# Three of the nine convolution taps formed on GpSimd and added once by VectorE, in nine of twelve channel blocks

## The reference

```python
def short_conv(x, w, grid):
    B, T, C = x.shape
    w = w.astype(jnp.float32)
    if grid:
        rows = T // GRID_W
        xg = jnp.pad(x.reshape(B, rows, GRID_W, C), ((0, 0), (1, 1), (1, 1), (0, 0)))
        out = sum(xg[:, i:i + rows, j:j + GRID_W, :] * w[i, j] for i in range(3) for j in range(3))
        return out.reshape(B, T, C)
    xp = jnp.pad(x, ((0, 0), (1, 1), (0, 0)))
    return sum(xp[:, j:j + T, :] * w[1, j] for j in range(3))

def rwkv_mixer(r, k, v, lw, la, lg, s0, grid, p):
    ...
    rkv = short_conv(jnp.concatenate([r, k, v], axis=-1), p['rw_conv'], grid)
    r, k, v = jnp.split(rkv, 3, axis=-1)
    g = jax.nn.sigmoid(lg) @ p['rw_g2']
    kk = heads(k * p['rw_k_k'])
    kk = kk * lax.rsqrt(jnp.sum(kk * kk, axis=-1, keepdims=True) + EPS)
```

## Time and profile before

| What | Value |
|---|---|
| Median of 3 runs | 957.44 us |
| Span of the profiled execution | 963.3 us |
| TensorE busy | 868.1 us, 90% of the span |
| VectorE busy | 562.5 us, 58% |
| ScalarE busy | 331.8 us, 34% |
| GpSimd busy | 151.6 us, 16% |
| Stage of the convolutions | about 197 to 386 us of the span |

### The profile page before, as it was taken

The page is one execution under the profiler, slowest core; times in us unless marked ns, Lnnn a source line. Parts: engine busy times, 40 slices in busy tenths (PEclk is TensorE's granted clock), DMA queues, the critical chain, the costliest instruction groups (busy, mean ns, idle before and its releaser), DMA issues.

```text
span 963.3 us, 21505 instructions
## 1 busy us (share of the span) xinstructions
PE 868.1 (90%) x8900; PEld 533.8 (55%) x8900; DVE 562.5 (58%) x935; ACT 331.8 (34%) x583; POOL 151.6 (16%) x296
## 2 busy tenths in 40 slices
PE   2899999999999979888888988899976899999995
PEld 1455455666455436577777877545565444444442
DVE  3424046699986899365665656686244255444467
ACT  3231111142035664566666553122110122222223
POOL 7000111112000106122223420000001000000041
PEclk9999999999999989899999999999955899999998
DMA  9902222224253102112212121961019499999956
GB/s 331 378 23 95 94 88 99 89 88 154 75 188 109 67 1 42 26 21 53 39 37 34 32 38 47 314 254 44 22 54 361 133 328 373 367 371 368 327 126 226
DMA packets 120816, 142.46 MB, mean 148 GB/s; under 512 B 49996, under 2 KB 86280, under 8 KB 120328
## 3 DMA queue, kind: packets, MB, share of 16 engines
q1 hardware_dynamic: 111880, 116.55, 36.9%
q0 software_dynamic: 3744, 13.63, 4.5%
q10 hardware_dynamic: 5088, 10.82, 3.0%
HBM read 122.99 MB, written 18.00 MB: 146 GB/s over the span
## 4 chain that ended last, share of the span: by engine, by line
PE 79%; DVE 10%; DMA 5%; issue 3%; ACT 3%; SPq 0%; ACTq 0%; DVEq 0%; POOLq 0%
PE bank L1972 72%; PE bank L1976 7%; DMA region<-in_w_ada_dram 3%; DVE rk_r L1431 1%; ACT region L949 1%; DMA region<-in_w_in_dram 1%; DMA rk_r<-h_rows_dram,slot_tokens 1%; DVE region L1431 1%; DVE rk_r L1432 1%; DVE cl_b L1890 1%; DVE region L1961 1%; ACT w_sb L949 1%; ACT ada_row_buffers L949 0%; DVE region L1957 0%; DVE region L1943 0%
## 5 line engine op out<-in xcount | busy, mean ns | idle before, releaser
L1972 PE MATMUL bank<-region 64*64 64x64 f32 (+3 forms) x3900 | 402.6, 299 | 16.4 <-issue 6.5
L1972 PEld LDWEIGHTS bank<-region 64*64 64x64 f32 (+1 forms) x3900 | 233.3, 149 | 171.6 <-issue 160.1
L949 ACT ACTIVATE region<-bank 128x256 f32<-128x256 f32 (+3 forms) x216 | 97.8, 453 | 357.7 <-PE bank L1972 261.1
L1972 PE MATMUL bank<-region,rk_r 128*128 128x512 f32 x176 | 81.0, 615 | 0.8 <-issue 0.8
L1976 PE MATMUL bank<-ident,region 128*128 128x128 f32 (+2 forms) x403 | 63.6, 289 | 15.1 <-DMA region<-in_c_dram 11.1
L1976 PEld LDWEIGHTS bank<-ident,region 128*128 128x128 f32 (+2 forms) x403 | 46.0, 146 | 33.6 <-issue 24.0
L1942 DVE TENSOR_SCALAR region<-region 128x256 f32<-128x256 f32 x16 | 4.7, 295 | 101.3 <-ACT region L949 101.3
L1431 DVE SCALAR_TENSOR_TENSOR rk_r<-region,vec,rk_r 128x512 f32<-128x512 f32 x64 | 50.1, 783 | 11.1 <-ACT rk_r L949 9.0
L1972 PEld LDWEIGHTS bank<-region,rk_r 128*128 128x128 f32 x176 | 34.0, 198 | 40.2 <-issue 39.0
L924 POOL DMA_INDIRECT rk_r<-h_rows_dram,slot_tokens x16 | 15.2, 949 | 248.9 <-PE bank L1976 132.8
L1972 PE MATMUL bank<-scratch,region 64*64 64x64 f32 (+1 forms) x688 | 43.8, 232 | 6.3 <-issue 3.4
(11 more groups left out here) (279 smaller groups left out, 1149.0 us busy)
## 6 DMA issues: line engine op xcount, KB each, us to landing
region<-in_moe_w_dram SPq DMA_DIRECT2D x38, 1024.0 KB, 10.2
region<-in_w_ada_dram SPq DMA_DIRECT2D x12, 2048.0 KB, 9.0
region<-in_w_in_dram SPq DMA_DIRECT2D x6, 2048.0 KB, 9.1
cl_b<-in_moe_w_dram SPq DMA_DIRECT2D x10, 1024.0 KB, 12.6
expert_rows_dram<-yg_b ACTq DMA_DIRECT2D x14, 512.0 KB, 6.8
region<-late_condition_dram SPq DMA_DIRECT2D x3, 1024.0 KB, 9.4
a_rows_dram<-region SPq DMA_DIRECT2D x20, 128.0 KB, 2.7
region<-inverse_rows_dram SPq DMA_DIRECT2D x20, 128.0 KB, 3.1
```

The lines of the kernel that those rows point to most:

```text
L949: return act.activation(out, in_, func, **kw)
L1972: return pe.matmul(out, lhsT, rhs, start=start, stop=stop)
```

## The change

For blocks 1 to 9 (r1 to v1) GpSimd computes the three taps of the lower neighbour row (the picture's rows 2 to 9) into a buffer, `last_row`: a tensor-scalar product for each tap and two additions, five instructions over 128 x 512. VectorE does five of its eight latent taps and adds `last_row` with one tensor-tensor addition. GpSimd starts a block when its first taps are there (`s_tap`) and VectorE has finished the block before (`s_conv`), since there is one `last_row` buffer. It lies in the room of the gate inputs, so ScalarE's copy of these waits until v1 is done. Blocks r0, v2 and v3 stay as they were.

```diff
+        last_row = lora_b[:, 2 * T:2 * T + LAT]
...
+            def third_row(n):
+
+                c_, dst, lat, line, out = conv_views(n)
+                pool.wait_ge(s_tap, c_ + 1)
+                pool.wait_ge(s_conv, c_)
+                one = vtok_b[:, 0:LAT] if n[0] == "v" else kk_b[:, 3 * T:3 * T + LAT]
+                acc_, one_ = (u.rearrange("p (y x) -> p y x", x=GW) for u in (last_row, one))
+                for j in range(3):
+                    own(pool.tensor_scalar(one_ if j else acc_, lat[:, 2:2 + GH, j:j + GW], tap(c_, 2, j), None, ALU.mult))
+                    if j:
+                        ins = pool.tensor_tensor(last_row, last_row, one, ALU.add)
+                        own(ins) if j == 1 else tell(ins, s_third)
...
             scaled_qk(4)
+            third_row("r1")
+            third_row("r2")
+            third_row("r3")
             pool.wait_ge(s_sig, 3)
...
-            for i in range(RC):
+
+            def squares(i):
                 pool.wait_ge(s_kk, i + 1)
                 tell(pool.tensor_tensor(sq[:, i], kkT[:, i], kkT[:, i], ALU.mult), s_prod)
+            third_row("k0")
...
+            third_row("v0")
+            squares(2)
+            squares(3)
+            third_row("v1")
...
+            act.wait_ge(s_conv, 2 * RC + 2)
             projected(slg, "lg")
...
-                for m in range(1, 9):
+                shared = 1 <= c_ < 2 * RC + 2
+                for m in range(1, 6 if shared else 9):
                     i, j = m // 3, m % 3
                     own(STT(out, lat[:, i:i + GH, j:j + GW], tap(c_, i, j), out, ALU.mult, ALU.add))
+                if shared:
+                    dve.wait_ge(s_third, c_)
+                    own(TT(dst[:, P:T], dst[:, P:T], last_row, ALU.add))
```

More of the change, by code:

```diff
@@ L435, in trunk_program @@
         s_tap = sem("first_taps")
+        s_third = sem("third_row_taps")
         s_slg = sem("gate_inputs_bounded")
@@ L851, in _ @@
             tell(pool.memset(raw_v, 0.0), s_rawz)
-            for i in range(RC):
+            def squares(i):
                 pool.wait_ge(s_kk, i + 1)
                 tell(pool.tensor_tensor(sq[:, i], kkT[:, i], kkT[:, i], ALU.mult), s_prod)
+            third_row("k0")
+            third_row("k1")
+            third_row("k2")
+            squares(0)
+            third_row("k3")
+            squares(1)
+            third_row("v0")
+            squares(2)
+            squares(3)
+            third_row("v1")
             def b_product(h):
```

## The result

The changed kernel took **976.11 us** (median of 4 runs, 973.32 to 978.4), the kernel before 957.08 on the same chip (4 runs): a ratio of 1.0203, 95% interval 1.0176 to 1.0229. It is slower by 19.0 us (16.8 to 21.9). The forecast was 964.6, with a range up to 971: the sign was right, the size was not.

The account below looks back on a forecast made before the run. The prediction took TensorE to bound the kernel, with VectorE mattering only at three waits. Its terms 0 (r and k blocks) + 2.6 (v0) + 4.6 (v1) = +7.2 us, added to 957.44, gave 964.6 us, range 959 to 971.

Parts of the forecast that it names:

- What bounds the kernel: Convolution stage: TensorE, busy 90% of the span, bounds it; a lighter VectorE pays only where TensorE stands still for it.
- the three waits named: TensorE's waits for the last gla_states(4), the copy behind v0 and a_and_b(0): 2.2, 2.7 and 3.8 us, 8.7 together.
- VectorE's 14.6 us: VectorE work saved over nine shared blocks, 1.6 us each: three taps fewer, one two-input pass more.
- VectorE was the bound: Rival: the stage follows VectorE's instruction list, so with half of 14.6 us hidden some 7 go: 950 us; chance 0.04.
- The tensor-scalar on GpSimd: One third-row product of 512 columns: 0.6 us, bounds 0.5 to 1.26; a third row 4.7 us, bounds 4.4 to 6.7.
- What GpSimd costs VectorE: Beside VectorE's taps, a two-input GpSimd instruction of 512 columns costs VectorE 0.85 us, a tensor-scalar 0.4.
- Who waits for whom in a block: Third row inside its own convolution: GpSimd ends with VectorE's five taps, 6.8 us; block 8.3 us against 7.0.
- Blocks r1 to r3: The stall in gla_states(4) from the gate's product only changes place: 0 us, bounds -2.2 to +1.1.
- Blocks k0 to k3: k3 ends later, but idle time ahead of v0 takes most of it: 0 us for TensorE, 0.5 handed on.
- Block v0: Its longer convolution and last two squares delay the copy TensorE waits for: +2.6 us, bounds +0.9 to +5.3.
- Block v1: Its third row stands ahead of b_product(0) on GpSimd, delaying TensorE's scores: +4.6 us, bounds +4.3 to +6.6.
- The rival with dear products: GpSimd's products take 1.26 us each and hold VectorE off for 0.85: the high ends, 970 us; chance 0.20.

Follow-up runs that it names:

- the kernel with two-input taps: Changed kernel with each third-row product on GpSimd a tensor-tensor, the tap repeated along the row, instead of a tensor-scalar: 976.57 us against 957.95 before.
- the kernel without k3: Changed kernel with k3, v0 and v1 convolved by VectorE alone; r1 to r3 and k0 to k2 stay shared: 961.93 us against 956.72 before.
- the two kernels without it ahead of the product: Changed kernel with v1's third row moved behind b_product(0) on GpSimd, 965.97 us; changed kernel with v1 convolved by VectorE alone, 966.98 us.

## Why the prediction was wrong in size

**What bounds the kernel: right.** TensorE's list is the spine, and 17 of the 19 us are in the three waits named. VectorE's 14.6 us were worth nothing; the rival "VectorE was the bound" is out.

**The tensor-scalar on GpSimd: the step that failed.** I took 0.6 us for one product, with 1.26, the two-input form, as the high end, and it takes 1.57. The bound rested on the thought that one input can't take longer than two, which no row showed. The third row becomes 3 x 1.57 + 2 x 1.27 + 4 x 0.1 = 7.65 us, not 4.7, and lies outside the bounds of 4.4 to 6.7. All that follows inherits it. The Trainium skill's statement that one-input operations run at roughly line rate (GPSIMD Engine Reference, 4.1 Engine selection), from which I had estimated 0.43 us, is off by more than a factor of three here.

**What GpSimd costs VectorE: right.** A tensor-scalar holds VectorE 0.3 us (0.4 taken), a two-input one of 512 columns about 0.8: in the kernel with two-input taps, 7.87 - 3.90 = 3.97 us for five. The tensor-scalar holds neither nothing, as the memset, nor its whole length, as I had read the contention that the Trainium skill names (GPSIMD Engine Reference, 1. Specifications): it holds a fifth of its length.

**Who waits for whom in a block: wrong.** "GpSimd ends with them" holds for a third row of 4.7 us. At 8.4, VectorE is done first and waits 2.9 to 4.3 us. k3 took 10.8 us with its square, where the forecast of 8.3 for a block and 0.85 for `squares(1)` makes 9.2.

**Blocks r1 to r3: 0 forecast, +2.1 us measured**, above the bound of +1.1. The stall did change its place, but r3's third row took 7.7 us, so the product started at 242.66, or 43.2 on the clock, instead of 238.3 (40.8), and all of its hold fell behind the last PSUM step. By the clock VectorE came to `gla_states(4)` 4.6 us sooner, lost 5.3 to the product and 1.4 to r3's additions: +2.1.

**Blocks k0 to k3: 0 forecast with 0.5 handed on, +3.8 us from k3.** k0 to k2 were hidden as forecast. Another 1.0 us is TensorE's own slower stretch in the kernel without k3, which no term of the forecast had.

**Block v0: +2.6 forecast, +1.0 to 1.4 measured** for its own sharing; the lateness came to it from k3.

**Block v1: the mechanism right, +4.6 forecast, +9.1 measured** (17.0 - 7.9 in the kernel after; 8.4 and 7.8 by the two kernels without it ahead of the product). The true third row adds 7.65 - 4.7 = 2.95. Two terms were missing: VectorE's step of line 1604 runs beside the second product and takes 1.8 us for 0.69, and TensorE's twelve matmuls behind the second wait took 0.3 more. With them the prediction's own sum comes to 4.6 + 2.95 + 1.1 + 0.3 = 8.95.

Together 2.1 (r blocks) + 1.0 (TensorE's stretch) + 3.8 (k3) + 1.0 (v0) + 9.1 (v1) = 17.0 us, against 7.2 forecast and 19.0 (16.8 to 21.9) measured. The terms come from single executions of different kernels, so each may be off by about 1 us. The rival with dear products, 970, was nearest, and its price was still too low.

## What to carry to other kernels

An operation that no row shows has no upper bound in its two-input sibling; where a whole forecast hangs on one such price, widen it or look for the case in which the engine becomes slower than the one it relieves. When work is given to a helper engine, look first at what stands behind it in that engine's list: moving one call behind the product that TensorE awaited gave half the loss back. And a block may be slowed for free only as far as idle time follows it; k3, the last of its row, had 0.28 us of it.

## What the hardware showed unexpectedly

On GpSimd, at 128x512 in float32, a tensor-scalar multiply took 1.57 us (1.49 with a constant), a tensor-tensor with both inputs full 1.27, and a tensor-tensor whose second input is one value repeated 1.04. So the one-input form was the slowest to run. It was also the gentlest neighbour: 0.3 us of VectorE's time lost for each, against about 0.8 for the two-input forms.
